# Expert stage of a hybrid decoder step: all six weight pieces split, 8 KB weight runs and strided transposes

## The reference, cut to what matters

```
def expert_block(args):
    xb, e = args                                    # xb: 128 x 1024
    hb = jax.nn.silu(xb @ w_gate[e]) * (xb @ w_up[e])   # 1024 x 512 each
    return hb @ w_down[e]                           # 512 x 1024
```

## Time and profile before

| | |
|---|---|
| median of 3 runs | 1961.63 us |
| the profiled execution | 1960.17 us, span 1958.6 us |
| granted TensorE clock, mean | 0.944 |
| PE busy | 1756.3 us, 90% of the span |
| DVE busy | 1158.8 us, 59% |
| ACT busy | 815.7 us, 42% |
| bytes over the span | 422.91 MB |
| packets under 2 KB, under 8 KB, all | 123168, 240344, 240657 |

### The profile page before, as it was taken

How to read it: one execution, slowest core, us unless ns; L and a number is a source line. 1 busy time by engine, 2 the same in 40 slices (tenths; PEclk the granted TensorE clock), 3 DMA queues, 4 the chain that set the end, 5 groups by cost and what they waited for, 6 DMA issues and landing times.

```text
span 1958.6 us, 28511 instructions
## 1 busy us (share of the span) xinstructions
PE 1756.3 (90%) x8894; PEld 1438.7 (73%) x8894; DVE 1158.8 (59%) x1669; ACT 815.7 (42%) x1444; POOL 317.0 (16%) x390
## 2 busy tenths in 40 slices
PE   2899999899999999999977997179999999999965
PEld 2899999688788788878746886067777777777742
DVE  5411110577777768867762332947777777777717
ACT  2332221344345435434311222136666666666623
POOL 1200000122322322232100111310000000000025
PEclk9999999899999999999966998579999999999978
DMA  6487521434423433333379225549999999999954
GB/s 208 144 256 204 171 70 50 140 100 144 143 91 115 159 123 104 120 105 101 98 240 319 75 106 198 189 162 381 399 399 397 399 399 397 399 400 397 348 200 187
DMA packets 240657, 422.91 MB, mean 216 GB/s; under 512 B 24976, under 2 KB 123168, under 8 KB 240344
## 3 DMA queue, kind: packets, MB, share of 16 engines
q1 hardware_dynamic: 187120, 321.93, 46.2%
q0 software_dynamic: 20048, 69.06, 10.1%
q10 hardware_dynamic: 33408, 30.94, 4.5%
HBM read 354.83 MB, written 78.55 MB: 221 GB/s over the span
## 4 chain that ended last, share of the span: by engine, by line
PE 35%; issue 7%; DVE 5%; DMA 1%; POOL 1%; ACT 1%; POOLq 0%; DVEq 0%; SPq 0%; ACTq 0%
PE PS L1922 8%; PE PS L1924 8%; PE PS L1923 8%; PE PS L2233 6%; PE PS L1929 2%; PE PS L2089 1%; PE PS L2096 1%; POOL hh L967 1%; PE PS L2119 1%; DVE zz L1894 1%; DVE ya L1906 0%; DMA yc<-obuf_dram,ridx 0%; PE PS L2201 0%; PE PS L2129 0%; DVE st L557 0%
## 5 line engine op out<-in xcount | busy, mean ns | idle before, releaser
L1789 DVE TENSOR_TENSOR wm_lo<-raw,wm_hi 128x2048 fp32r<-128x2048 f32 x156 | 352.0, 2289 | 147.8 <-ACT wm_hi L1299 147.7
L1299 ACT CAST wm_hi<-raw 128x2048 fp32r<-128x2048 f32 x160 | 301.6, 1907 | 75.7 <-PE PS L1924 75.7
L1922 PE MATMUL PS<-w_hi,hT_hl 128*128 128x512 f32 (+1 forms) x584 | 233.5, 400 | 13.8 <-DMA hT_hl<-hl_dram 9.1
L1923 PE MATMUL PS<-w_lo,hT_hl 128*128 128x512 f32 (+1 forms) x584 | 227.5, 390 | 0.0
L1924 PE MATMUL PS<-w_hi,hT_hl 128*128 128x512 f32 (+1 forms) x584 | 227.1, 389 | 0.0
L1922 PE MATMUL PS<-wm_hi,xT_hi 128*128 128x512 f32 x512 | 204.0, 398 | 3.1 <-DVE xT_lo L1854 3.1
L1924 PE MATMUL PS<-wm_hi,xT_lo 128*128 128x512 f32 x512 | 201.2, 393 | 0.0
L1923 PE MATMUL PS<-wm_lo,xT_hi 128*128 128x512 f32 x512 | 200.9, 392 | 0.0
L1962 PE MATMUL PS<-xa_hi,wn 128*128 128x384 f32 x480 | 162.8, 339 | 0.2 <-ACT ev L1074 0.2
L1964 PE MATMUL PS<-xa_hi,wn 128*128 128x384 f32 x480 | 162.2, 338 | 0.0
L1963 PE MATMUL PS<-xa_lo,wn 128*128 128x384 f32 x480 | 162.2, 338 | 0.0
(11 more groups left out here) (345 smaller groups left out, 3332.9 us busy)
## 6 DMA issues: line engine op xcount, KB each, us to landing
raw<-in_w_gate SPq DMA_DIRECT2D x64, 1024.0 KB, 8.7
raw<-in_w_up SPq DMA_DIRECT2D x64, 1024.0 KB, 10.0
raw<-in_w_down SPq DMA_DIRECT2D x64, 1024.0 KB, 10.2
hT_hl<-hl_dram POOLq DMA_DIRECT2D x70, 512.0 KB, 5.2
braw<-in_w_in SPq DMA_DIRECT2D x16, 1024.0 KB, 6.3
obuf_dram<-yb ACTq DMA_DIRECT2D x32, 512.0 KB, 6.9
nd_dram<-ev ACTq DMA_DIRECT2D x72, 192.0 KB, 2.7
nd<-nd_dram SPq DMA_DIRECT2D x36, 384.0 KB, 3.7
```

What stands on the lines that cost most here:

```text
L1299: act.copy(wm_hi[:, j], raw[:, j]).then_inc(m_hi[j // 4], 1)
L1789: dve.tensor_tensor(wm_lo[:, j], raw[:, j], BF(wm_hi[:, j]), ALU.subtract).then_inc(m_lo[j // 4], 1)
L1922: pe.matmul(out, x_hi, w_hi_, start=start, stop=False)
L1923: pe.matmul(out, x_hi, w_lo_, start=False, stop=False)
```

## The change

- All six pieces are split. `wm_hi` and `wm_lo` have six buffers instead of five, `raw` six instead of seven: piece 5 is no longer double-buffered and is read by ACT and DVE instead of PE. ACT's and DVE's steps each have one more piece.
- `down` is 24 split products instead of 12 and four unsplit ones. `hT_f` goes; `hT_hi` and `hT_lo` hold all 512 columns.
- The block's output is copied by ACT alone, in one copy of 1024 columns; DVE's half and its semaphore `m_yd` go.
- Weight rows go to partitions in runs: row p*k + i to partition p. A piece is then one run of 8 KB for each partition, in DRAM and in SBUF. To match, the transposes take columns with a stride of 8 (x) and 4 (hm) elements.
- Three h1 blocks instead of one are loaded after the loop, since the space is taken.

More of the change, by code:

```diff
@@ L273, in build @@
     hm = sb(sE, "hm", [P, DE])
-    hT_hi = sb(sE, "hT_hi", [P, DE // 2], F32R)
-    hT_lo = sb(sE, "hT_lo", [P, DE // 2], F32R)
+    hT_hi = sb(sE, "hT_hi", [P, DE], F32R)
+    hT_lo = sb(sE, "hT_lo", [P, DE], F32R)
     yb = [sb(sE, f"yb{s}", [P, D]) for s in range(2)]
[L277 to L281, removed]
+    wm_hi = sb(sE, "wm_hi", [P, 6, 2048], F32R)
+    wm_lo = sb(sE, "wm_lo", [P, 6, 2048], F32R)
+    h1l = sb(sE, "h1l", [P, NB - 3, D])
+    raw = sb(sE, "raw", [P, 6, 2048])
     st = raw[:, 0:4].rearrange("p g (n e) -> p g n e", n=NS)
@@ L287, in build @@
     yc = sb(sF, "yc", [P, NB, D])
-    h1e = sb(sF, "h1e", [P, D])
+    h1e = sb(sF, "h1e", [P, 3, D])
     zz = [sb(sF, f"zz{s}", [P, D]) for s in range(2)]
@@ L424, in build @@
     m_lo = [ssem(f"m_lo{i}") for i in range(2)]
-    m_raw = [sem(f"m_raw{s}") for s in range(2)]
     m_used = [ssem(f"m_used{i}") for i in range(2)]
@@ L432, in build @@
     m_ya = ssem("m_ya")
-    m_yd = ssem("m_yd")
     m_yo = [dsem(f"m_yo{s}") for s in range(2)]
@@ L468, in piece_hi @@
     def piece_hi(t, j):
-        return (m_hi[0], upto(4 * t + j)) if j < 4 else (m_hi[1], upto(t))
+        return (m_hi[0], upto(4 * t + j)) if j < 4 else (m_hi[1], upto(2 * t + j - 4))
     def piece_lo(t, j):
-        return (m_lo[0], upto(4 * t + j)) if j < 4 else (m_lo[1], upto(t))
+        return (m_lo[0], upto(4 * t + j)) if j < 4 else (m_lo[1], upto(2 * t + j - 4))
     def piece_used(t, j):
@@ L785, in o_step, with m_load @@
             h_load(b + 1, 1 - s)
-        def m_load(e, j, dst, landed):
+        def m_load(t, e, j):
             src = A[("w_gate", "w_up", "w_down")[j // 2]][0]
             kc, half = (KC, j % 2) if j < 4 else (DE // P, j % 2)
-            v = src[ds(e, 1)].rearrange("o (k p) n -> p (o k) n", p=P)
+            v = src[ds(e, 1)].rearrange("o (p k) n -> p (o k) n", p=P)
             v = v[:, half * kc // 2:(half + 1) * kc // 2, :]
-            sp.dma_start(raw[:, dst].rearrange("p (k n) -> p k n", k=kc // 2), v).then_inc(landed, 16)
+            sp.dma_start(raw[:, j].rearrange("p (k n) -> p k n", k=kc // 2), v).then_inc(w_raw[j], 16)
         h_load(0, 0)
@@ L803, in _ @@
         sp.wait_ge(s_out, 16 * (G + 2))
-        for j in range(5):
-            m_load(0, j, j, w_raw[j])
-        m_load(0, 5, 5, m_raw[0])
+        for j in range(6):
+            m_load(0, 0, j)
         h1_store(7, 1)
@@ L810, in f_load @@
         def f_load(b):
-            sp.dma_start(h1l[:, b] if b < NB - 1 else h1e[:], h1_dram[b * P:(b + 1) * P, :]).then_inc(f_h[b][0], 16)
+            sp.dma_start(h1l[:, b] if b < NB - 3 else h1e[:, b - NB + 3], h1_dram[b * P:(b + 1) * P, :]).then_inc(f_h[b][0], 16)
         for s in range(2):
@@ L815, in _ @@
         sp.wait_ge(o_lg, upto(8))
-        for b in range(NB - 1):
+        for b in range(NB - 3):
             f_load(b)
@@ L823, in m_up @@
                 sp.wait_ge(*piece_lo(t - 1, j))
-                m_load(e, j, j, w_raw[j])
-        def m_down(t, s):
+                m_load(t, e, j)
+        def m_down(t):
             e = t if isinstance(t, int) else sp.value_load(etab[0:1, ds(t, 1)], min_val=0, max_val=NE - 1)
-            sp.wait_ge(*piece_lo(t - 1, 4))
-            m_load(e, 4, 4, w_raw[4])
-            sp.wait_ge(*piece_used(t - 2, 5))
-            m_load(e, 5, 5 + s, m_raw[s])
+            for j in (4, 5):
+                sp.wait_ge(*piece_lo(t - 1, j))
+                m_load(t, e, j)
         m_up(1)
-        m_down(1, 1)
+        m_down(1)
         m_up(2)
         m_up(3)
-        m_down(2, 0)
+        m_down(2)
         sp.wait_ge(d_route, 1)
@@ L842, in _ @@
             m_up(2 * i + 4)
-            m_down(2 * i + 3, 1)
+            m_down(2 * i + 3)
             m_up(2 * i + 5)
-            m_down(2 * i + 4, 0)
-        m_down(2 * iters + 1, 1)
-        sp.wait_ge(m_yd, upto(2 * iters + 1))
+            m_down(2 * i + 4)
+        m_down(2 * iters + 1)
+        sp.wait_ge(m_ya, upto(2 * iters + 1))
         sp.wait_ge(m_x[0], 16 * (iters + 2))
@@ L1011, in _ @@
         last = 2 * iters + 1
-        pool.wait_ge(m_yd, upto(last))
+        pool.wait_ge(m_ya, upto(last))
         wait_apart(pool, m_yo[0], 16 * (iters + 2))
@@ L1845, in _ @@
         iters = 15 + (dve.value_load(novr[0:1, 0:1], min_val=0, max_val=16) + 1) // 2
[L1847 to L1850, removed]
         def x_low(t):
@@ L1881, in _ @@
         m_step(2 * iters + 1, 1, iters, True, False)
-        y_half(2 * iters + 1, 1, iters)
         dve.wait_ge(m_yo[0], 16 * (iters + 2))
         dve.wait_ge(m_yo[1], 16 * (iters + 2))
-        dve.wait_ge(*piece_lo(2 * iters + 1, 4))
+        dve.wait_ge(*piece_lo(2 * iters + 1, 5))
         def f_sum(b, s):
@@ L1893, in f_sum @@
             q = 2 * (b % 4)
-            dve.scalar_tensor_tensor(zz[s][:], h1l[:, b] if b < NB - 1 else h1e[:], ALPHA, PS[:, q:q + 2].rearrange("p a n -> p (a n)"),
+            dve.scalar_tensor_tensor(zz[s][:], h1l[:, b] if b < NB - 3 else h1e[:, b - NB + 3], ALPHA, PS[:, q:q + 2].rearrange("p a n -> p (a n)"),
                                      ALU.mult, ALU.add).then_inc(f_z, 1)
@@ L2216, in up, with down @@
                     last.then_inc(m_used[j // 4], 1)
-        def down(t, s, uses):
+        def down(t):
             pe.wait_ge(m_hlo, upto(t))
             pe.wait_ge(m_ya, upto(t - 1))
-            pe.wait_ge(m_yd, upto(t - 1))
-            pe.wait_ge(*piece_lo(t, 4))
-            for k in range(2):
+            for k in range(DE // P):
+                j = 4 + k // 2
+                if k % 2 == 0:
+                    pe.wait_ge(*piece_lo(t, j))
                 for half in range(2):
-                    c = k * D + half * 512
+                    c = (k % 2) * D + half * 512
                     last = split_product(PS[:, 5 + half], hT_hi[:, k * P:(k + 1) * P], hT_lo[:, k * P:(k + 1) * P],
-                                         wm_hi[:, 4, c:c + 512], wm_lo[:, 4, c:c + 512], k == 0, False)
-            last.then_inc(m_used[1], 1)
-            pe.wait_ge(m_raw[s], 16 * (uses + 1))
-            for k in range(2):
-                for half in range(2):
-                    c = k * D + half * 512
-                    last = pe.matmul(PS[:, 5 + half], hT_f[:, k * P:(k + 1) * P], raw[:, 5 + s, c:c + 512],
-                                     start=False, stop=(k == 1))
-            last.then_inc(m_used[1], 1)
+                                         wm_hi[:, j, c:c + 512], wm_lo[:, j, c:c + 512], k == 0, k == DE // P - 1)
+                if k % 2 == 1:
+                    last.then_inc(m_used[j // 4], 1)
         def x_transposes(t, s, uses):
@@ L2239, in x_transposes, with m_step @@
             pe.wait_ge(t_lo, upto(NB + t - 1))
-            transposes(0, xw[s], KC).then_inc(t_T, 1)
-        def m_step(t, s, uses, before, prev, more):
+            strided_transposes(0, xw[s], KC).then_inc(t_T, 1)
+        def m_step(t, s, uses, prev, more):
             pe.wait_ge(t_lo, upto(NB + t))
@@ L2251, in m_step @@
             if prev:
-                down(t - 1, 1 - s, before)
+                down(t - 1)
             pe.wait_ge(m_hm, upto(t))
             pe.wait_ge(m_hlo, upto(t - 1))
-            transposes(4, hm, DE // P).then_inc(u_T, 1)
+            strided_transposes(4, hm, DE // P).then_inc(u_T, 1)
         x_transposes(0, 0, 0)
-        m_step(0, 0, 0, None, False, True)
+        m_step(0, 0, 0, False, True)
         with pe.Fori(0, iters) as i:
[L2260 to L2263, removed]
+            m_step(2 * i + 1, 1, i + 1, True, True)
+            m_step(2 * i + 2, 0, i + 1, True, True)
+        m_step(2 * iters + 1, 1, None, True, False)
+        down(2 * iters + 1)
         pe.wait_ge(m_ya, upto(2 * iters + 1))
-        pe.wait_ge(m_yd, upto(2 * iters + 1))
         for b in range(NB):
```

## The result

The changed kernel takes 1941.45 us (median of 5 runs, 1935.38 to 1943.94) against 1961.19 for the kernel before beside it (5 runs, 1954.66 to 1962.73): a ratio of 0.990, 95% interval 0.988 to 0.992. The forecast was 1942. The profiled execution took 1938.04 us, span 1936.2.

A forecast was written before the change was run, and what follows sets the result against it. PE was taken to pace the expert stage, with DMA nearly a second limit. -22.6 + 1.9 + 0.2 + 0.6 = -19.9 us from 1960.17 gave 1940.3; the runs' median lay 1.46 above, so 1942 us, range 1937 to 1964.

The forecast's parts named there:

- What bounds the kernel: Expert stage, 32 blocks: PE paces at 18.41 us a step, DMA at 399 GB/s is nearly a second limit.
- Down on PE, -0.73 us a step: Down in each block: four unsplit matmuls (3.43 us) become 12 split ones (2.70 us), step 17.68 us.
- the 22.6 of the sum: Expert stage: the saving from down's split over the 31 steps that contain a down, -22.6 us.
- 8 KB rows, 424 GB/s: Weight loads: longer runs move 424 GB/s or a little more, 17.3 us a block at most, under PE.
- The carried-on trend to 443: Weight loads: upper bound for 8 KB runs, from the 2 KB and 4 KB rates carried on, 443 GB/s.
- Strided transposes at nothing: x and hm transposes on PE: strided weight loads, ten in chains a step, cost nothing extra.
- R1: Rival, transposes: strided weight load at half rate, 46 ns more each, 0.46 us a step, 1956 us; chance 0.26.
- R2: Rival, transposes: strided load takes four times as long, 1.38 us a step, 1985 us; chance 0.11.
- ACT and DVE: Each step with one more piece: ACT 14.7 us, DVE 16.3 us, DVE 1.4 us to spare, nothing late.
- Last block, +1.9: Last block: exposed piece 5 +2.5, last down -0.9, single output copy +0.3, together +1.9 us.
- Edges: Outside the loop: ACT's sixth initial cast +0.2 us, three h1 blocks loaded at the end +0.6 us.
- The late h1 loads: After the loop: 1 MB more beside the gathers, needed only by the last sums, +0.6 us, between 0 and 2.6.

The follow-up runs named there:

- e1: The changed kernel with the old row layout (runs of 2 and 4 KB) and contiguous transposes: 1957.85 us, ratio 0.9994.
- e2: The kernel before with the new row layout and strided transposes, down still with its unsplit piece: 1959.13 us, ratio 1.0001.
- e3: The changed kernel with contiguous instead of strided transposes on the new rows (numbers then not the reference's): 1947.6 us in one run.
- e7: The changed kernel without down's product hT_lo x wm_hi, a third of down: 1929.21 us in one run.
- e8: The changed kernel with 4 KB runs in gate and up, x transposed with a stride of two elements, hm contiguous: 1942.22 us, ratio 0.9902.
- e6: The changed kernel with an unused DVE maximum over 2048 elements added to each step: 1943.05 us in one run.
- e6c: The changed kernel with two unused DVE maxima, over 2048 and over 512 elements, added to each step: 1961.27 us in one run.
- e5: The changed kernel with e4's last-block order and the three late h1 loads behind the first gather: 1937.43 us, ratio 0.9897.
- e4: The changed kernel with the last block's piece 5 split after hT instead of ahead of it: 1941.38 us, ratio 0.9904.

## Why the prediction was right

**What bounds the kernel.** Right, and the sentence that carried it is "A shorter step therefore pays only if DMA becomes faster too": e1 and e2 show each half without effect, and both together save 1%. One reading was too small and changes nothing: 54.8 us is one of four rows of ACT's waits for PE, 176 us together.

**Down on PE, -0.73 us a step.** 0.654 measured. Of the missing 0.08, 0.046 is the stride (e3). The rest is pitch: I priced the 12 added products at up's 0.225, a mean that holds a first gap of 0.11, and the added ones stand 0.227 apart, which over 12 of them is 0.03. I counted 31 steps; 30 lie between first and last silu and one is in the tail. All this makes the 22.6 of the sum 20.3 (31 x 0.654).

**8 KB rows, 424 GB/s.** Right as a rate that suffices, and its ceiling is 422 (e7). That it came so near is partly luck: I had read 424 as the rate of 4 KB rows, and e8, with 4 KB rows alone, moves 412 while its landings grow. The carried-on trend to 443 that I kept as a bound was nowhere seen.

**Strided transposes at nothing.** The choice was right to 0.05 us a step, the reading beside it was wrong. I took the 23 ns that 64 columns add in a chain for 46 ns of exposed load per 128. The loads did become 48 to 66 ns longer and only some 4 ns of each reached the step (0.046 over the twelve). What I timed were the loads' own rows, and loads run ahead of their products; besides, the eight of the earlier trace rows are two groups of four with a handover between them. The products (timeline of PE in the kernel before) take no less time with 64 weight columns than with 128, 0.63 against 0.60 us for a group of four, and behind the first gap of a group both start 109 to 110 ns apart. So the chain's pitch did not hang on the load:

```profile
1031.72 0.63 PE L2113 MATMUL PS<-ident,Kw 128*64 128x128 f32 x4
...
1620.95 0.60 PE L1929 MATMUL PS<-ident,hm 128*128 128x128 f32 x4
```

It hangs on longer loads a little: at 189 ns the pitch is still 108 to 113, at 206 and 207 about 120. So R1 had the load's price right and its place on the path wrong, and 0.26 was too much for it. R2's factor of four, which no row had shown, was nowhere seen. The Trainium skill, SBUF — State Buffer, Door 1, says that an access which needs a new 16-byte line for each element loses rate. The loads' own rows agree at 32 and 16 bytes (189 and 206 ns against 141), but at 8 bytes, two elements to a line, where by the page the rate is kept, the row shows 207.

**ACT and DVE.** Right that nothing is late; the spare of DVE was at least 2.2 us instead of 1.4 (e6, e6c), since I added up rows that overlap.

**Last block, +1.9.** PE's idle time is the 4.52 us that I had at 4.8, and the copy is 1.01 us. Mis-sized is the last down: -0.9 was predicted for it, and it takes 7.96 us (1856.70 to the copy at 1864.66) against 8.04 before. The windows of after show why: the granted clock is 0.50 and 0.52, the lower of its two levels (1.2 GHz), for 4.7 us behind the idle time, and ten products stand 0.43 apart instead of 0.23.

```profile
1856.60:1859.00 2.40, 2.30 (x6) 1.82 (x7) 0.00 (x0) 0.00 (x0) 0.00 (x0) 0.50 0.31 125
1859.00:1861.50 2.50, 2.50 (x8) 1.98 (x7) 0.00 (x0) 0.00 (x0) 0.00 (x0) 0.52 0.00 0
1861.50:1864.60 3.10, 3.10 (x14) 2.25 (x12) 0.00 (x0) 0.00 (x0) 0.00 (x0) 1.00 0.00 0
```

The price that I started from held such a stretch too: 12 split products took 4.41 us in before, against 2.63 in a step. In e2, behind the same 2.27 us of idle time, the clock stayed at the upper level and the whole last down took 6.48 us. So 1.6 us of the tail hang on the clock in one execution (windows of before, then of e2):

```profile
1880.60:1884.60 4.00, 3.98 (x11) 3.15 (x12) 0.00 (x0) 0.00 (x0) 0.00 (x0) 0.58 0.34 135
```

```profile
1885.00:1889.00 4.00, 4.00 (x15) 2.89 (x16) 0.00 (x0) 0.00 (x0) 0.00 (x0) 1.00 0.32 131
```

**Edges.** The start is right: ACT's sixth cast delays rt_e, and DVE's operation on it (timeline, as the earlier trace rows) still ends with POOL's subtraction, both at 1229.3. From the router's last cast on DVE (idx_all) to the first silu it is 19.63 us against 19.45.

```profile
1224.75 4.51 POOL L977 TENSOR_TENSOR wm_lo<-raw,wm_hi 128x2048 fp32r<-128x2048 f32 x1 [10.97 <-ACT wm_hi L1295]
...
1226.61 2.67 DVE L1776 TENSOR_SCALAR rt_s<-rt_e 128x9 f32<-128x9 f32 x1 [2.11 <-ACT rt_e L1300]
```

The late h1 loads were priced at 0.6: from the first gather's issue to the first final product 9.72 us became 11.84, so 2.1, inside the bound of 2.6. I had called them needed only by the last sums; what they delayed were the gathers beside them: in e5, which holds them back, the first final product comes 8.34 us behind the first gather's issue. Of these 3.5 us 2.0 are lost again behind the third sum, where one small operation of DVE takes 2.31 us instead of 0.15 while POOL is at work.

By the forecast's own terms the tail should have lost about 1.8 (1.9 + 0.6, less 0.73 for the down in it) and lost 3.1, and the steps won less than the sum has. That the median met 1942 within a microsecond owes something to time ahead of the stage, which no step of mine named.

## What to carry to other kernels

When the engine that paces is level with a second resource, compute the rate that the shorter step asks of that resource, and change both or neither: either half alone measures as nothing and would be thrown away. A longer record of an operation that another hides is no longer step; ask what the chain's pitch does, not what the row lasts. A piece handled like all others in the steady loop can stand exposed in the last pass: look there for a second, cheaper order.

## What the hardware showed that I had not expected

- A weight load of 128 columns takes 141 ns contiguous, 189 with elements 32 bytes apart, 206 at 16 bytes and 207 at 8. In a chain, transposes start 109 ns apart contiguous, 108 to 113 at 32 bytes and about 120 at 16 and 8.
- The kernel's DMA mix moves 399 GB/s with 2 KB rows in gate and up and 4 KB in down (e1) and 422 with 8 KB (e7), where it is the bound in both; with 4 KB in all six (e8) it moves the 412 that the step asks, with growing landings.
- Two runs in which PE was idle for 1.81 us ahead of the last down differ in what followed: in e4 the granted clock was 0.54 from 1863.5 to 1866, in e5 1.00 from 1857.4 to 1860. Before and e2 differ in the same way after 2.27 us (0.58 and 1.00). Why, no run here tells.
- Code that is the same reached its first silu up to 9.6 us apart in eight profiles, half of what the change is worth; a step read from the trace is 17.753 us in six of them.
